# Late choices of experts: four units side by side at the seam of dense stage and tail, six in pairs that share their waits

## The reference, cut to what matters

```python
q = (h @ w_q).reshape(B, S, 8, 2, 128)
s1 = einsum('bshd,hnd->bshn', q[..., 0, :], k1)      # 128 scores
s2 = einsum('bshd,hnd->bshn', q[..., 1, :], k2)      # 128 scores
v1, i1 = top_k(s1, 16);  v2, i2 = top_k(s2, 16)
cand = v1[..., :, None] + v2[..., None, :]           # 16 x 16
vs, ic = top_k(cand, 16)
e = i1[ic // 16] * 128 + i2[ic % 16]                 # 16 experts
w = softmax(vs)
act = gelu(u[e] . h) * w                             # per token, head, expert
y = sum(act * vt[e])                                 # rows of 2048
```

## Time and profile before

| | us |
|---|---|
| median of three runs | 3549.25 (3537.24 to 3550.75) |
| the profiled execution | 3551.22 |
| its span, first to last instruction | 3549.5 |
| its dense stage | about 2287 to 2961 |
| its tail | about 2975 to 3525 |

### The profile page before, as it was taken

How to read it: one execution, slowest core, us unless ns; L and a number is a source line. 1 busy time by engine, 2 the same in 40 slices (tenths; PEclk the granted TensorE clock), 3 DMA queues, 4 the chain that set the end, 5 groups by cost and what they waited for, 6 DMA issues and landing times.

```text
span 3549.5 us, 39077 instructions
## 1 busy us (share of the span) xinstructions
PE 2994.6 (84%) x14684; PEld 2295.2 (65%) x14684; DVE 2497.3 (70%) x3426; ACT 1159.7 (33%) x1759; POOL 608.5 (17%) x692
## 2 busy tenths in 40 slices
PE   5599997999989997999799999799999995444445
PEld 1288885546768885659699899688888883211112
DVE  3889984655757775547664545598989995877777
ACT  1421224414224234233554634344444441111101
POOL 0000000000100000000000000122222225766663
PEclk9899999999998998999899999899999997767778
DMA  8556672161765784437443444599999998989997
GB/s 324 208 225 237 253 268 107 61 236 75 294 248 217 294 315 158 154 119 281 181 156 143 159 150 155 220 409 412 406 411 410 414 398 317 377 347 366 360 360 287
DMA packets 149477, 932.67 MB, mean 263 GB/s; under 512 B 21552, under 2 KB 30000, under 8 KB 40880
## 3 DMA queue, kind: packets, MB, share of 16 engines
q0 software_dynamic: 77568, 520.24, 37.8%
q1 hardware_dynamic: 57616, 384.82, 27.5%
q10 hardware_dynamic: 14112, 25.17, 1.9%
HBM read 900.79 MB, written 29.36 MB: 262 GB/s over the span
## 4 chain that ended last, share of the span: by engine, by line
PE 51%; DVE 21%; DMA 8%; PEld 7%; issue 6%; ACT 3%; POOL 2%; another core or an unknown queue 1%; DVEq 0%; ACTq 0%; SPq 0%; PEldq 0%; POOLq 0%
PE psum L959 21%; PE psum L931 16%; PEld psum L959 7%; DVE psum L2037 6%; PE psum L966 5%; DMA memr<-in_panels_dram 4%; DVE w_lo L1227 3%; PE psum L1105 3%; DVE junk L1633 3%; DMA memr<-in_ada_dram 2%; PE psum L1122 2%; ACT w_hi L1221 1%; PE psum L1113 1%; POOL memh L826 1%; POOL memr L838 1%
## 5 line engine op out<-in xcount | busy, mean ns | idle before, releaser
L1227 DVE TENSOR_TENSOR w_lo<-memr,w_hi 128x1024 fp32r<-128x1024 f32 x614 | 737.5, 1221 | 397.5 <-ACT w_hi L1221 394.4
L1221 ACT ACTIVATE w_hi<-memr 128x1024 fp32r<-128x1024 f32 x614 | 641.4, 1056 | 930.0 <-PE psum L959 328.1
L959 PE MATMUL psum<-h_hi,w_hi 128*128 128x512 f32 (+1 forms) x1696 | 604.8, 357 | 77.1 <-DVE h_lo L1714 43.9
L1633 DVE CUSTOM_DVE_ANT_0 junk<-memr 128x2048 bf16<-128x2048 f32 x240 | 548.9, 2287 | 119.1 <-DMA memr<-in_ada_dram 77.4
L959 PE MATMUL psum<-h_lo,w_hi 128*128 128x512 f32 (+1 forms) x1696 | 590.4, 348 | 0.0
L959 PE MATMUL psum<-h_hi,w_lo 128*128 128x512 f32 (+1 forms) x1696 | 590.2, 348 | 0.0
L1144 PE MATMUL psum<-memr,memh 128*128 128x512 f32 x480 | 248.1, 678 | 312.6 <-ACT memh L1575 207.1
L959 PEld LDWEIGHTS psum<-h_hi,w_hi 128*128 128x128 f32 x1696 | 325.4, 192 | 135.2 <-issue 64.8
L931 PE MATMUL psum<-w_hi,l_hi 128*128 128x512 f32 x1024 | 399.6, 390 | 13.5 <-DVE w_lo L1227 12.9
L931 PE MATMUL psum<-w_lo,l_hi 128*128 128x512 f32 x1024 | 398.9, 390 | 0.0
L931 PE MATMUL psum<-w_hi,l_lo 128*128 128x512 f32 x1024 | 398.9, 390 | 0.0
(11 more groups left out here) (230 smaller groups left out, 4231.1 us busy)
## 6 DMA issues: line engine op xcount, KB each, us to landing
memr<-in_panels_dram SPq DMA_DIRECT2D x339, 1024.0 KB, 6.9
memr<-in_ada_dram POOLq DMA_DIRECT2D x176, 1024.0 KB, 6.0
dots<-sq ACTq DMA_DIRECT2D x64, 256.0 KB
memr<-in_xin_dram SPq DMA_DIRECT2D x1, 4096.0 KB, 14.0
gstore<-sq ACTq DMA_DIRECT2D x16, 256.0 KB
memh<-gstore SPq DMA_DIRECT2D x2, 2048.0 KB, 7.5
memr<-gstore SPq DMA_DIRECT2D x2, 2048.0 KB, 9.6
memr<-in_xin_dram SPq DMA_DIRECT2D x2, 2048.0 KB, 10.1
```

Of the source, the lines that this page charges most:

```text
L959: ins = pe.matmul(bank(o["bank"])[:, 0:o["w"]], w_[:, c, :], x_[:, kc, :], start=kc == 0 and j == 0, stop=kc == DC - 1 and j == 2)
L1221: act.activation(w_hi[:, m % HALVES, :, :], slot[:, 8 * i:8 * i + 8, :], ACT.Copy).then_inc(hi_ready, 1)
L1227: dve.tensor_tensor(w_lo[:, m % HALVES, :, :], raw_panel(o["g"])[0][:, 8 * i:8 * i + 8, :], w_hi[:, m % HALVES, :, :].bitcast(F32), ALU.su ...
L1633: chain(dve.tensor_tensor_reduce(junk[:, :], w, cact[:, v_, :], 1.0, 0.0, ALU.mult, ALU.add, mod[:, a, m:m + 1]))
```

## The change

In words: the small buffers exist four times (`choice_buffers`; three further sets lie in memory that is free in the tail). `top16` and the choosing functions take a list of units: each step is done for all units of the list, and only then comes the stop. The copies of the scores and of the token offset into buffers are dropped; the instructions read them where they are. In the experts' step both halves are compared side by side (8 stops for 11). The units in SEAM (tail units 2 to 5) get their keys and pairs at the start of the tail, ahead of `coefficients(0)`, all four side by side, and their experts during m = 0, two at the third row and two at the seventh. The other six are chosen in pairs during m = 1, 3 and 5 (PAIRS), with their pieces at the same rows as before; the other m choose nothing. ACT does the four exponentials of SEAM ahead of the first gelu, and those of a pair ahead of the gelu of the next unit. The units chosen in the dense stage are still chosen one by one.

```diff
@@ -770,25 +770,31 @@
             small_at[0] += int(np.prod(shape))
             return v if dt is F32 else v.bitcast(dt)
 
-        s12 = small(2, P)
-        s12b = small(2, P)
-        cand = small(S)
-        candb = small(S)
-        v16 = small(2, TOPK)
-        i16 = small(2, TOPK, dt=U32)
-        i16f = small(2, TOPK)
-        vs = small(TOPK)
-        ic = small(TOPK, dt=U32)
-        ab = small(2, TOPK, dt=U32)
-        abf = small(2, TOPK)
-        e16 = small(2, TOPK)
+        def choice_buffers(small):
+
+            return dict(left=small(2, P), v16=small(2, TOPK), i16=small(2, TOPK, dt=U32), i16f=small(2, TOPK),
+                        cand=small(S), candb=small(2, S), vs=small(TOPK), ic=small(TOPK, dt=U32), ab=small(2, TOPK, dt=U32),
+                        abf=small(2, TOPK), e16=small(2, TOPK), nvs=small(4), vexp=small(TOPK))
+
+        def late_small(*shape, dt=F32):
+            v = region(late_at[0], *shape)
+            late_at[0] += int(np.prod(shape))
+            return v if dt is F32 else v.bitcast(dt)
+
+        late_at = [HL + 2048]
+        buffers = [choice_buffers(small)] + [choice_buffers(late_small) for _ in range(3)]
+        assert late_at[0] <= HL + 8192
         wgt = small(2 * HEADS, TOPK)
-        nvs = small(4)
-        tok = small(1)
         act16 = small(2, TOPK)
         gel16 = small(TOPK)
         coef = small(TOPK)
-        vexp = small(TOPK)
+
+        SEAM = tuple(range(EARLY + 2, EARLY + 6))
+        PAIRS = {1: tuple(range(EARLY + 6, EARLY + 8)), 3: tuple(range(EARLY + 8, EARLY + 10)),
+                 5: tuple(range(EARLY + 10, EARLY + 12))}
+        buffers_of = {n: buffers[0] for n in range(EARLY + 2)}
+        for units in (SEAM,) + tuple(PAIRS.values()):
+            buffers_of.update(zip(units, buffers))
 
         assert small_at[0] <= AR + 6144
 
@@ -1506,7 +1506,8 @@
         def act_wexp(act, n):
 
             act.wait_ge(vs_ready, n + 1)
-            act.activation(vexp[:, :], vs[:, :], ACT.Exp, bias=nvs[:, 0:1], accum_out=nvs[:, 1:2]).then_inc(wexp_ready, 1)
+            b = buffers_of[n]
+            act.activation(b["vexp"], b["vs"], ACT.Exp, bias=b["nvs"][:, 0:1], accum_out=b["nvs"][:, 1:2]).then_inc(wexp_ready, 1)
 
         LAST = EARLY_STEPS * (EARLY - 1)
         CHOICES = {0: (0, 2), 1: (0, 3)}
@@ -1530,11 +1531,11 @@
...
-                choose_keys(dve, unit, piece, chain)
+                choose_keys(dve, [unit], piece, chain)
...
-                choose_pairs(dve, unit, chain)
+                choose_pairs(dve, [unit], chain)
...
-                choose_experts(dve, unit, chain)
+                choose_experts(dve, [unit], chain)
...
@@ -1575,10 +1576,12 @@
                     act.activation(diags[:, q % DIAGS, :], ident, ACT.Identity,
                                    scale=late_coefs[:, m, j:j + 1]).then_inc(diag_ready, 1)
 
+            for n in SEAM:
+                act_wexp(act, n)
             weigh(0)
             for m in range(LATE):
-                if m + 2 < LATE:
-                    act_wexp(act, EARLY + m + 2)
+                for n in PAIRS.get(m, ()):
+                    act_wexp(act, n)
                 if m + 1 < LATE:
                     weigh(m + 1)
 
@@ -1689,8 +1692,8 @@
...
-                choose_keys(dve, st["choose"], 0, chain)
-                choose_keys(dve, st["choose"], 1, chain)
+                choose_keys(dve, [st["choose"]], 0, chain)
+                choose_keys(dve, [st["choose"]], 1, chain)
...
@@ -1959,52 +1962,85 @@
...
+        def top16(dve, link, parts):
...
+            for s, left, v, ix in parts:
+                ins = dve.max(v[:, 0:8], s)
+            link(ins)
...
+            for s, left, v, ix in parts:
+                dve.max_index(ix[:, 0:8], v[:, 0:8], s)
+                ins = dve.match_replace(left, v[:, 0:8], s, -3e38)
+            link(ins)
...
+            for s, left, v, ix in parts:
+                ins = dve.max(v[:, 8:16], left)
+            link(ins)
...
+            for s, left, v, ix in parts:
+                ins = dve.max_index(ix[:, 8:16], v[:, 8:16], left)
+            link(ins)
+
+        def choose_keys(dve, units, a, link):
+
+            top16(dve, link, [(scores[:, n, P * a:P * a + P], buffers_of[n]["left"][:, a, :], buffers_of[n]["v16"][:, a, :],
+                               buffers_of[n]["i16"][:, a, :]) for n in units])
+
+        def choose_pairs(dve, units, link):
+
+            bs = [buffers_of[n] for n in units]
+            for b in bs:
+                dve.tensor_copy(b["i16f"], b["i16"])
+                ins = dve.tensor_tensor(b["cand"].rearrange("p (a b) -> p a b", a=TOPK),
+                                        b["v16"][:, 0, :].unsqueeze(2).broadcast_to([P, TOPK, TOPK]),
+                                        b["v16"][:, 1, :].unsqueeze(1).broadcast_to([P, TOPK, TOPK]), ALU.add)
+            link(ins)
+            top16(dve, link, [(b["cand"], b["candb"][:, 0, :], b["vs"], b["ic"]) for b in bs])
+            for b in bs:
+                dve.tensor_scalar(b["nvs"][:, 0:1], b["vs"][:, 0:1], -1.0, None, ALU.mult).then_inc(vs_ready, 1)
+
+        def choose_experts(dve, units, link):
+
+            bs = [buffers_of[n] for n in units]
+            for b in bs:
+                dve.tensor_scalar(b["ab"][:, 0, :], b["ic"], 4, None, ALU.logical_shift_right)
+                ins = dve.tensor_scalar(b["ab"][:, 1, :], b["ic"], 15, None, ALU.bitwise_and)
+            link(ins)
+            for b in bs:
+                ins = dve.tensor_copy(b["abf"], b["ab"])
+            link(ins)
+            for a in range(2):
+                eqs = [b["candb"][:, a, :].rearrange("p (k j) -> p k j", k=TOPK) for b in bs]
+                for b, eq in zip(bs, eqs):
+                    ins = dve.tensor_tensor(eq, b["abf"][:, a, :].unsqueeze(2).broadcast_to([P, TOPK, TOPK]),
+                                            con("iota", TOPK).unsqueeze(1).broadcast_to([P, TOPK, TOPK]), ALU.is_equal)
+            link(ins)
+            for a in range(2):
+                for b in bs:
+                    eq = b["candb"][:, a, :].rearrange("p (k j) -> p k j", k=TOPK)
+                    ins = dve.tensor_tensor(eq, eq, b["i16f"][:, a, :].unsqueeze(1).broadcast_to([P, TOPK, TOPK]), ALU.mult)
+            link(ins)
+            for a in range(2):
+                for b in bs:
+                    ins = dve.reduce_sum(b["e16"][:, a, :], b["candb"][:, a, :].rearrange("p (k j) -> p k j", k=TOPK), AX_X)
+            link(ins)
+            for b in bs:
+                ins = dve.scalar_tensor_tensor(b["abf"][:, 0, :], b["e16"][:, 0, :], float(N_KEYS), b["e16"][:, 1, :],
+                                               ALU.mult, ALU.add)
+            link(ins)
+            for n, b in zip(units, bs):
+                dve.tensor_copy(idx[:, n, :], b["abf"][:, 0, :])
+                ins = dve.tensor_scalar(b["abf"][:, 1, :], b["abf"][:, 0, :], tokens[:, n, :], None, ALU.add)
+            link(ins)
+            for n, b in zip(units, bs):
+                dve.tensor_copy(eidx[:, n, :], b["abf"][:, 1, :]).then_inc(idx_ready, 1)
+            dve.wait_ge(wexp_ready, units[-1] + 1)
+            for b in bs:
+                ins = dve.reciprocal(b["nvs"][:, 2:3], b["nvs"][:, 1:2])
+            link(ins)
+            for n, b in zip(units, bs):
+                dve.tensor_scalar(wgt[:, n, :], b["vexp"], b["nvs"][:, 2:3], None, ALU.mult)
...
@@ -2016,18 +2052,23 @@
...
+            for a in range(2):
+                choose_keys(dve, SEAM, a, chain)
+            choose_pairs(dve, SEAM, chain)
             coefficients(0)
             for m in range(LATE):
...
                 for i, j in enumerate(DVE_ROWS):
...
-                    if m + 2 < LATE and i in (2, 4):
-                        choose_keys(dve, EARLY + m + 2, i // 4, chain)
-                    if m + 2 < LATE and i == 6:
-                        choose_pairs(dve, EARLY + m + 2, chain)
-                    if m + 2 < LATE and i == 8:
-                        choose_experts(dve, EARLY + m + 2, chain)
+                    if m == 0 and i in (2, 6):
+                        choose_experts(dve, SEAM[i // 2 - 1:i // 2 + 1], chain)
+                    if m in PAIRS and i in (2, 4):
+                        choose_keys(dve, PAIRS[m], i // 4, chain)
+                    if m in PAIRS and i == 6:
+                        choose_pairs(dve, PAIRS[m], chain)
+                    if m in PAIRS and i == 8:
+                        choose_experts(dve, PAIRS[m], chain)
...
```

More of the change, by code:

```diff
@@ L879, in build @@
         one_t = sb("one_t", [P, 1])
[L881 to L884, removed]
         def pe_gemm(pe, st):
@@ L1960, in dve_mixed @@
             dve_normed2(dve, 1)
-        def top16(dve, link, s, sb_, v, ix):
+        def top16(dve, link, parts):
             dve.sem_inc(held_dve, 1)
-            link(dve.max(v[:, 0:8], s))
+            for s, left, v, ix in parts:
+                ins = dve.max(v[:, 0:8], s)
+            link(ins)
```

(36 more changed lines are left out.)

## The result

| | before | after |
|---|---|---|
| median, beside each other | 3541.91 us (3537.24 to 3550.75) | 3560.84 us (3554.78 to 3564.07) |
| profiled execution | 3551.22 | 3554.78 |
| its span | 3549.5 | 3552.8 |

What follows compares the result with a forecast made beforehand. In the tail a loop of DVE, POOL and DMA engines around 12 row slots limits, with DVE's lateness stopping the DMA. Saving 33 us, less 13 for late DVE instructions, gives -20: 3529 us, range 3511 to 3557.

Steps and rivals of the forecast that it cites:

- So a unit whose DMA never stops takes 46.5 - 4.5 = 42 us: Tail, steady stretch: a unit takes 46.5 us, of which the DMA engines stand still 4.5, leaving 42.
- The rule for the stop: Tail: DMA stop equals issue of row 8 minus landing of the next dots + 1.8 us; 2.7 gives 4.5.
- each stop is added to 42: Tail: a unit's time is 42 us plus its DMA stop, taken as the cost of DVE's lateness.
- the -33 us: Tail: saving if no stretch of late DVE instructions intervenes; dots of unit 11 at 3464 against 3497.4.
- if plain units still take 46 us: Tail units without choices: at that pace the forecast is wrong, since DMA or POOL was the bound.
- 38.7, yet a unit takes 46.5: Tail: DVE's 26.3 us of rows plus 12.4 of choices, against the unit's time; the rest laid to slow DVE instructions.
- POOL's 32 issues at 1.25 make 40, below that: Tail: POOL's issue takes 40 us a unit, below the 42 of a unit whose DMA never stops.
- The episodes: Tail: DVE's short instructions come 1.4 us apart instead of 0.46; two of three doubled units hit, 5.5 + 7.6 = 13 us.
- The cost of doubling: Two units' choices in one: 19.0 us on DVE, stops of 2.4 in unit 1 and 1.4 in units 3 and 5.
- rival 3: Choices: sharing waits brings nothing, an instruction costs what it cost alone; +27 us, 3556; chance 0.08.
- Rival 1: Tail: no stretch of late DVE instructions, or one; 3516 us, with one 3523; chance 0.26.
- Rival 4: Tail: late stretches come by the number of DVE instructions, not by unit; 7 x 7.6 = 53 us, 3569; chance 0.10.

Runs made afterwards that it cites:

- the run without choices: Kernel before with the ten late choices left out, later tail units reusing unit 1's experts and weights (another output): 3532.46 us, ratio 0.9978.
- the run with the early seam: Changed kernel, but DVE's choices at the seam wait for PE alone, for ACT only ahead of the first coefficients: 3558.82 us, ratio 1.0051 to before.
- the single order with the new functions: Kernel before's schedule, one unit chosen per tail unit, with the changed kernel's choosing functions: 3537.86 us, 0.9995; on another chip 3496.72 us, 0.9996.
- half of the dots: 8 of 16 dots gathered per tail unit, each used for two rows (another output): ratio to before 0.9961 and 0.9960 in before, 0.9990 in after.
- the zero matmuls: Matmuls of zeros behind PE's tail rows to keep PE busy: ratio to before 1.0041 and 1.0043 in after, 1.0010 in the old order with new functions.

## Why the prediction was wrong

- **"So a unit whose DMA never stops takes 46.5 - 4.5 = 42 us"** is right as a number (41.1 in the run without choices, 42.7 and 42.9 in after). The rule for the stop looked at one of POOL's two waits only. Ahead of the row at 3361.2 it had already waited 4.0 us for the experts of unit 9, so in this unit of before DVE's lateness did hold POOL, for 7.0 us:

```profile
3357.27 0.94 POOL L826 DMA_INDIRECT memh<-dots,memr  x1 [3.98 <-DVE memr L2004]
```

- **The step that failed** is the next, "each stop is added to 42" with DVE's lateness as its only source: the stops were laid to the choices. They also come in units without any (45.0 in after, 43.9 without choices), and where a chip has none, the units with choices take 41. So the -33 us wasn't there to be had: leaving out every late choice brought 8. The last line of the prediction had named the sign, "if plain units still take 46 us".
- **"38.7, yet a unit takes 46.5"**: the conclusion that DVE's loop sets it was the error behind that. 38.7 was below POOL's 40 and the 41 to 42 of the DMA engines. POOL is hardly ahead of them: in the windows of 4 us around its stop at 3339.3 they ran dry within some 5 us of its last issue, so what is longer in a pause of POOL goes to the end. "POOL's 32 issues at 1.25 make 40, below that" dismissed it, though a pause of 2 us in it is enough to make it the slowest.
- **The episodes** in the doubled units came about as forecast and aren't what broke the sum: in after DVE's short instructions lost 8.7 us in unit 1, 2.0 in unit 3 and 7.6 in unit 5, 18.3 for the forecast's 13. Not in the sum was the one at the seam, 9.4. In plain rows it was POOL that stopped, and DVE's rows ran on.
- **The cost of doubling** was in the sum, as stops of 2.4 and 1.4 us, but set against a gain. It is what is left: 1.2 us at the seam (2.5 forecast; 10 on the first chip with its episode, which the run with the early seam shows to be of no account there), 2.5 in unit 0 and 3.8 in units 1 and 2; then 0.3 back, 4.6 with the half's sum, and 0.3 over the rest. Together 12.1 between the two traces on the chip without stops. The stop rule looked at row 8 only; POOL waited at the row behind the pairs as well.
- **Right**: the parts' sizes, the start at the seam, DVE's 45.3 us in a doubled unit, and the chance against rival 3: a doubled unit takes DVE 45.4, where two units' choices at their single cost would make 26.3 + 2 x 12.4 = 51. Rival 1 fell with the gain it kept. Rival 4 named a time in the right direction (3569). Its cause isn't needed for a loss: on a chip with no episode 9.9 us of median are lost. Whether episodes add to that on the first chip, where it is 18.9, isn't shown; the intervals of the two ratios overlap.

## What to carry to other kernels

An engine that idles 5% in a loop is not its bound, even if it is the busiest: add up each engine's and queue's own pace for one turn (here DVE 38.7, POOL 40, DMA 41 to 42) before pricing work on one of them. The quick test is to leave the work out and time it: it costs one run and would have put the gain at some 8 us (2 to 13) at most. Work hidden under another pace must stay spread evenly, since batching it to save waits puts it over the limit in some turns and pays little back in the others. No version here that computes the same beat the kernel before beyond its interval; the single order with the new functions equals it (0.9995 and 0.9996).

## What the runs showed of the hardware

- Chips differ: the same kernel takes 3541.9 and 3540.7 us on chips 7 and 2 (and 3541.9 in the first comparison), 3500.8 and 3498.7 in two sessions on chip 8 and 3497.8 on chip 9. All of it is in the tail, 563.0 against 513.9 us in the traces. On the slower ones the DMA engines move 396 to 398 GB/s in windows of it that no stop falls into (after, 3345 to 3385; without choices, 3308 to 3366), on chip 8 mostly 409 to 411.
- On the slower chips POOL stops for 3 to 9 us, in plain stretches of after every 44 issues (60 to 62 us), in the run without choices 38 to 58 issues apart, three times followed by another 6 issues on. All ten in that run, and five in after (at 3151.6, 3213.9, 3339.3, 3399.6 and 3461.0), are at a row whose slot PE read last. PE was done with it 2 us before the wait began at 3339.3 in after, and 8 us before it at 3374.2 in the run without choices. The cause is open. That POOL waits for new instructions finds no support: no packet of the instruction queues moved in those five stops of after, and in the run without choices only two of the ten begin within 1 us of one (at 3368 and 3449).
- On the same chips DVE's short instructions come late, by up to 5.3 us at once (after, 3072.85), with POOL stopped or not, and its rows aren't touched. With half of the dots or the zero matmuls neither was seen, but nor was it in the unchanged kernels on those chips; on a slower chip these edits didn't run.
